# First group of the gated-delta layer: two weight panels and the gate weights read the residual times the norm's weights, and the root is multiplied in behind PSUM

## The reference

```python
x = x + rmsnorm(ff, g_post_mlp)                       # end of the first block (norm "nB")
hn = rmsnorm_2(h, pre_norm[layer])                    # norm "n3": h * rsqrt(mean(h*h) + eps) * pre_norm
proj = hn @ w_in                                      # q, k, v, z (panels) and b, a (gates)
qkv = silu(causal_depthwise_conv(qkv, conv_w))        # four taps per channel
beta = sigmoid(b)
g = -exp(a_log) * softplus(a + dt_bias)               # decays; gc = cumsum(g) within chunks of 64
```

## Time and profile before

| what | value |
|---|---|
| median of 3 runs | 1941.73 us (1940.2 to 1943.67) |
| the profiled execution | 1942.34 us, its span 1939.6 us |
| PE busy | 1833.5 us, 95% of the span |
| DVE, ACT, POOL busy | 994.7, 822.8, 676.4 us |
| the stretch of the change | about 742 to 800 us of the span |

### The profile page before, as it was taken

How to read it: one execution, slowest core, us unless ns; L and a number is a source line. 1 busy time by engine, 2 the same in 40 slices (tenths; PEclk the granted TensorE clock), 3 DMA queues, 4 the chain that set the end, 5 groups by cost and what they waited for, 6 DMA issues and landing times.

```text
span 1939.6 us, 30688 instructions
## 1 busy us (share of the span) xinstructions
PE 1833.5 (95%) x11693; PEld 1538.4 (79%) x11829; DVE 994.7 (51%) x1753; ACT 822.8 (42%) x1503; POOL 676.4 (35%) x429
## 2 busy tenths in 40 slices
PE   6999999999999998998999999999978999999996
PEld 4777788888787876887989998998976667777776
DVE  6522233731111225665765774775766556566666
ACT  4566643352323233633633642562445443333433
POOL 3222244453534342270280263255224212222312
PEclk9999999999999998999999999999999999999998
DMA  5112133232323230420230131122132101221201
GB/s 186 55 55 66 55 98 109 66 98 68 118 80 105 86 99 21 137 79 1 80 89 23 55 91 48 52 80 78 34 111 76 55 33 55 65 55 53 76 32 44
DMA packets 73668, 138.90 MB, mean 72 GB/s; under 512 B 30640, under 2 KB 42416, under 8 KB 73296
## 3 DMA queue, kind: packets, MB, share of 16 engines
q1 hardware_dynamic: 72976, 132.41, 22.7%
q10 hardware_dynamic: 576, 4.87, 0.6%
HBM read 127.62 MB, written 9.63 MB: 71 GB/s over the span
## 4 chain that ended last, share of the span: by engine, by line
PE 44%; DVE 6%; POOL 5%; issue 3%; ACT 3%; DMA 0%; SPq 0%; ACTq 0%; POOLq 0%; DVEq 0%
PE ps L348 9%; PE ps L350 8%; PE ps L349 8%; PE ps L3092 4%; PE ps L3048 2%; POOL wsp L343 2%; PE ps L3055 2%; PE ps L3082 1%; POOL ov L836 1%; PE ps L2770 1%; POOL work L832 1%; PE ps L2874 1%; PE ps L2907 1%; PE ps L2912 1%; DVE aux_f L1789 1%
## 5 line engine op out<-in xcount | busy, mean ns | idle before, releaser
L343 POOL TENSOR_TENSOR wsp<-raw,wsp 128x1024 fp32r<-128x1024 f32 x228 | 549.8, 2418 | 1154.7 <-ACT wsp L338 1154.5
L348 PE MATMUL ps<-h_split,wsp 128*128 128x264 f32 (+2 forms) x1552 | 535.0, 345 | 16.8 <-DVE h_split L497 5.0
L349 PE MATMUL ps<-h_split,wsp 128*128 128x264 f32 (+2 forms) x1552 | 516.0, 332 | 0.0
L350 PE MATMUL ps<-h_split,wsp 128*128 128x264 f32 (+2 forms) x1552 | 515.6, 332 | 0.0
L348 PEld LDWEIGHTS ps<-h_split,wsp 128*128 128x128 f32 x1552 | 294.3, 190 | 58.2 <-issue 17.2
L349 PEld LDWEIGHTS ps<-h_split,wsp 128*128 128x128 f32 x1552 | 295.3, 190 | 28.8 <-issue 0.2
L350 PEld LDWEIGHTS ps<-h_split,wsp 128*128 128x128 f32 x1552 | 294.2, 190 | 29.2
L338 ACT ACTIVATE wsp<-raw 128x1024 fp32r<-128x1024 f32 x228 | 237.6, 1050 | 95.2 <-PE ps L350 94.5
L348 PE MATMUL ps<-y_split,wsp 128*128 128x512 f32 (+2 forms) x512 | 196.4, 384 | 11.5 <-DVE y_split L531 5.3
L349 PE MATMUL ps<-y_split,wsp 128*128 128x512 f32 (+2 forms) x512 | 192.5, 376 | 0.0
L350 PE MATMUL ps<-y_split,wsp 128*128 128x512 f32 (+2 forms) x512 | 192.0, 375 | 0.0
(11 more groups left out here) (391 smaller groups left out, 2929.6 us busy)
## 6 DMA issues: line engine op xcount, KB each, us to landing
raw<-in_w SPq DMA_DIRECT2D x228, 512.0 KB, 3.5
m_home<-ov SPq DMA_DIRECT2D x16, 256.0 KB, 3.5
x_home<-x_res ACTq DMA_DIRECT2D x1, 2112.0 KB, 6.9
x_res<-in_x SPq DMA_DIRECT2D x4, 512.0 KB, 5.3
out<-x_res SPq DMA_DIRECT2D x16, 128.0 KB, 1.7
x_res<-x_home ACTq DMA_DIRECT2D x1, 1584.0 KB, 7.4
mats<-in_mats SPq DMA_DIRECT2D x1, 640.0 KB, 7.4
x_res<-x_home ACTq DMA_DIRECT2D x1, 528.0 KB, 3.9
```

Of the source, the lines that this page charges most:

```text
L343: pool.tensor_tensor(wsp[:, s, 1, :], raw[:, s, :], wsp[:, s, 0, :].bitcast(F32), ALU.subtract).then_inc(lo_ready, 1)
L348: pe.matmul(o, wh, xh, start=start, stop=False)
L349: pe.matmul(o, wh, xl, start=False, stop=False)
L350: return pe.matmul(o, wl, xh, start=False, stop=stop)
```

## The change

The norm "n3" gets two versions. The first is without the root: while `norm_add` still runs, ACT rounds `X` times the norm's weights into `Y` (tile `y_split`; `gained_high`, L526), and DVE makes its correction (`low_plain`, L531) two additions behind. With it PE computes panels 0 and 1 and the gate weights, in between the sums of squares. The root is multiplied in as DVE takes the results from PSUM: `rows_rooted` for the gates, `tile_rooted(0)` and `tile_rooted(1)` for the two tiles, into `QKV` (in tile `work`), from where the taps then read. The second version is with the root, as before, into `HS`, for panel 2 and all behind (`scaled_whole`, `high_whole`, `low_whole`); its small scratch moves from `ov` to `work` (`N3`). The gates' steps stand at other places, ACT's `split_high` of panels 2 and 3 stands between the squares, half of tile 3 stands ahead of the decay rows. Semaphore counts move along.

```diff
--- before.py
+++ after.py
+        N3 = dict(sq=(F[:, 4224:4752], F[:, 4752:5280]), rs=F[:, 6864:7392], tmp=(F[:, 7392:7920], F[:, 7920:8448]))
...
+        ROOTED = (0, 1)
...
-        def norm_add(dve, tag, src, gain, N, c, rs):
+        def norm_add(dve, tag, src, gain, N, c, rs, after=None):
...
+                if after is not None and kt >= 2:
+                    after(kt - 2)
+            if after is not None:
+                after(KT - 2)
+                after(KT - 1)
...
@@ ACT @@
-            norm_squares(act, "n3", lambda k: X[:, k, :], N2, ready=lambda k: added("nB", k))
-            norm_rsqrt(act, "n3", N2, True)
-            norm_high(act, "n3", N2, hs(ALL))
+            for k in range(KT):
+                norm_square(act, "n3", lambda k: X[:, k, :], N3, k, lambda k: added("nB", k))
+                gained_high(act, "n3", k, Y[:, 0, k, :], X[:, k, :], "pre_norm_0")
+                if k in (2, 4):
+                    split_high(act, P_GDN + AHEAD + k // 2 - 1)
+            norm_rsqrt(act, "n3", N3, True)
...
-                split_ahead(0)
                 if first:
-                    gates_front()
-                    split_ahead(1)
-                    gates_middle()
+                    for k in range(KT):
+                        high_whole(k)
+                        if k == 5:
+                            gates_middle()
                     conv_exp(0)
                     decay_high()
...
@@ DVE @@
-            norm_add(dve, "nB", lambda k: acc1[:, k, :], "g_post_mlp", N1, REAL, PS[:, 7, :])
...
-            norm_apply(dve, "n3", lambda k: X[:, k, :], "pre_norm_0", N2, hs(ALL))
+
+            def low_plain(k):
+                gained_low(dve, "n3", k, Y[:, 1, k, :], X[:, k, :], "pre_norm_0", Y[:, 0, k, :])
+            norm_add(dve, "nB", lambda k: acc1[:, k, :], "g_post_mlp", N1, REAL, PS[:, 7, :], low_plain)
...
+            def rows_rooted():
+                dve.wait_ge(sem("ba_pe"), 1)
+                dve.tensor_tensor(two(ba_f[0:32, :]), PS[0:32, 6:8, 0:HALF], two(N3["rs"][0:32, :]), ALU.mult)\
+                   .then_inc(sem("ba_dve"), 1)
+
+            def tile_rooted(t):
+                dve.wait_ge(used, P_GDN + t + 1)
+                dve.tensor_tensor(two(QKV[:, t, :]), acc2(2 * t), two(N3["rs"]), ALU.mult)\
+                   .then_inc(sem("norm_branch"), 1)
...
+                    scaled_whole(0)
+                    scaled_whole(1)
+                    for k in range(2, KT):
+                        low_whole(k - 2)
+                        scaled_whole(k)
+                        if k == 3:
+                            rows_rooted()
+                        if k == 5:
+                            gates_front()
+                            tile_rooted(0)
+                        if k == 6:
+                            gates_end()
+                    low_whole(KT - 2)
+                    low_whole(KT - 1)
                     taps(0)
-                    gates_front()
+                    tile_rooted(1)
                     conv_clamp(0)
                     decay_low()
...
@@ PE @@
-            norm_mean(pe, "n3", N2, True)
...
                     ready(0)
+                    ready(1)
+                    for kt in range(KT):
+                        square_sum(kt)
+                        if kt % 2:
+                            plain(0, kt // 2)
+                            plain(1, kt // 2)
                     for kt in range(KT):
...
-                        last = mm3t(pe, 6, *w, HS, kt, kt == 0, kt == KT - 1)
...
-                        last = mm3t(pe, 0, *part(0, kt), HS, kt, kt == 0, kt == KT - 1)
+                        last = mm3t(pe, 6, *w, Y, kt, kt == 0, kt == KT - 1)
+                    last.then_inc(sem("ba_pe"), 1)
+                    for kt in range(4, KT):
+                        plain(0, kt)
+                    gates_turned()
+                    for kt in range(4, KT):
+                        plain(1, kt)
+                    pe.wait_ge(*rooted(0))
+                    ready(2)
+                    for kt in range(KT):
+                        pe.wait_ge(*whole_ready(kt))
+                        last = mm3t(pe, 0, *part(2, kt), HS, kt, kt == 0, kt == KT - 1)
+                        if kt == 4:
+                            decay_sums()
                     last.then_inc(used, 1)
-                    project(1, 2, 0, 3)
-                    gates_turned()
-                    project(1, 2, 3, 6)
-                    decay_sums()
-                    project(1, 2, 6)
-                    pe.wait_ge(sem("g_conv"), 1)
-                    project(2, 0)
+                    pe.wait_ge(*rooted(1))
+                    project(3, 2, 0, 4)
                     pe.wait_ge(sem("rows_moved"), 16 + 64)
...
                     decay_rows(5, 4).then_inc(sem("g_gr"), 1)
-                    pe.wait_ge(sem("g_conv"), 2)
-                    project(3, 2, 0, 4)
```

95 lines of the change are left out of this document (63 added, 32 removed).

## The result

The changed kernel takes 1953.62 us (median of 9 runs, 1946.81 to 1957.44); the kernel before, on the same chip, 1943.44 (1940.2 to 1947.43). The ratio is 1.0048, with a 95% interval of 1.0037 to 1.0059: slower by 9.3 us, where 4.1 were forecast. All three say slower, each by less than half a per cent; their mean, weighted by their intervals, is 1.0040, 7.8 us. The kernel before itself lies 1.7 to 2.4 us above the 1941.73 from which the forecast counted: that was the median of its first three runs, and samples of 9 to 35 runs give 1943.44 to 1944.12.

A forecast was written before the change was run, and what follows sets the result against it. It took the chain through norm n3 and the decays, not PE, as the bound: root 3.8 us late, collision 4.4, `decay_low` 4.3 late, +4.1 at `l2_scale(1)`, so 1945.8 us. Range 1940.3 to 1949.3.

The forecast's parts named there:

- The corrections and the root: At norm n3: DVE's eight corrections between the additions make POOL's last addition and the root 3.8 us later.
- The collision: First two scalings on DVE wait for POOL's two back-to-back panel splits: 4.4 us, bounds 0 and 4.8.
- above 2 us each: Sign that the forecast is right: each of the first two scalings of `h_split` on DVE takes over 2 us.
- From the second scaling to `decay_low`: DVE's scalings, corrections, gate steps and taps, then conv's exponential on ACT: `decay_low` ends at 785.3, 4.3 us late.
- The decays' way and the first row: The decays' way through DRAM takes 8.56 us as before, so PE's first decay row comes at 793.9.
- PE's clock there: Low clock expected when `l2_sum(0)` starts at 797.3; 5.9 us to `l2_sum(1)`; `l2_scale(1)` ends at 806.4, +4.1.
- Behind it nothing takes the shift back: After `l2_scale(1)`, DVE's queue, M through DRAM and POOL's elimination keep the same steps, so the +4.1 us stays.
- The two waits of PE: Sign that the forecast is right: PE idle 5 us before the decay rows and 2 to 3 behind.
- PE the bound: Rival, chance 0.10: tile 2 ends 4.1 us earlier and the wait for the decays closes; 1937.6, faster.
- No collision: Rival, chance 0.10: scalings run beside the splits, or splits come earlier; all behind 4.4 earlier; 1941.4, no change.
- Slack behind: Rival, chance 0.13: decays are 4 us late, but taps and panels behind have room; 0 to 1.5 us arrive; 1942.5.
- PE slow from the start: Rival, chance 0.07: squares and half tiles leave PE at 1.2 GHz, all is 9 us late; 1950.7.

The follow-up runs named there:

- early splits: Changed kernel with panels 2 and 3 split on ACT and POOL ahead of the norm's additions; median 1943.71 us, ratio interval 0.9994 to 1.0021.
- the delay: Kernel before with seven unused products (4.8 us) more on DVE between the root of n3 and the first scaling; ratio 1.0033.
- decays first: Changed kernel with the decays' small steps ahead of taps and conv's exponential, both groups of Abs ahead of that of tile 1; 1950.28 us.
- matmuls in the wait: Changed kernel with 44 unused matmuls more on PE between the first half of tile 3 and the decay rows; its time is not given in the text.

## Why the prediction was right or wrong

The direction and the mechanism of the stretch were right, the size was not: +4.1 us were forecast, +7.8 measured (+5.6, +7.8 and +9.3 in three measurements). The step that failed is the end of the sum: it takes the +4.1 at `l2_scale(1)`, worked out against one profile, for the whole difference, with the work behind put at +0 ("the same steps"), and adds it to the median of three runs. The runs showed in its place +5.0 at `l2_scale(1)` against that profile, +5.4 against the mean of two, +7.8 in the time, and a start 1.7 to 2.4 above 1941.73.

- *The corrections and the root*: 3.8 late forecast, 3.5 measured. POOL's additions and DVE's corrections held each other up, as foreseen for the last: 1.75 us for POOL's (1.28 in the earlier trace rows), 2.47 for the two corrections beside it (eight took 5.52 where no addition ran). Right in size. But that last addition was one of three, and all took 1.75, not only the last.
- *The collision*: 4.4 forecast; 4.2 by the early splits, which take it away. Here both scalings ended after the second split, as the upper bound said, because the copy of `cwg` took the slot between the splits (2.29 us). The rule of the Trainium skill (SBUF — State Buffer, "SBUF: two separate sides") foretold this order, and the trace agrees with it. The pair ended at (766.9), where the sum had 767.3. Right, and the term that decided; only the sign "above 2 us each" failed, since the copy paid for one of the two waits and the second scaling took 0.76.
- *From the second scaling to `decay_low`*: 785.3 forecast, (785.28) measured. That it is right to 0.1 is in part luck: from the pair's end 18.0 were forecast and 18.3 measured, which made up for the pair's 0.4.
- *The decays' way and the first row*: 793.9 forecast, (794.2). Nearly right: the way through DRAM took 8.8 to 9.0 us in the three profiles instead of 8.56. "This is the step that decides" was only half right: taken forward by 3.6 us, the decays gave back 0.5 to 1.4, because DVE's taps and the ACT work behind them are as late.
- *PE's clock there*: the low level came as forecast, the times with it were a little too small. I had 5.9 us from the start of `l2_sum(0)` to that of `l2_sum(1)`; it was 6.2 (6.4 and 5.7 in the other profiles), and from the first row to `l2_sum(0)` it was 3.78 instead of 3.4 (the prediction's own rows give 3.55). `l2_scale(1)` was forecast at 806.4, and measured (807.3), (807.7) and (806.8).
- *The kernel before as the measure*: I took one profile of it, with the clock lower behind the norm than in its repeat (0.50 against 0.68 from 760 to 764). Against the mean of the two, the stretch is later by 4.9 to 5.8, 5.4 in the mean, instead of 4.1. In the same way its first three runs were a low sample of its time.
- *"Behind it nothing takes the shift back"*: right, shown by the delay. It also doesn't shrink: 4.0 to 4.9 us in the stretch came with a ratio of 1.0033 (+4.1 to +8.7 us).
- *The two waits of PE*, 5 and 2 to 3 us, were 6.36 and 2.98. That nothing lies over the second was right. That this costs was wrong: with the half tile put back there `l2_sum(0)` starts 2.3 later and `l2_sum(1)` at the same time.
- *The rivals.* PE the bound: refuted, PE idled 6.36 ahead of the rows. No collision: refuted by the copy and the pair. Slack behind: refuted by the delay. PE slow from the start: refuted, its clock was 1.00 from 764 to 770, where the kernel before had just come up.

Of +7.8, then, 5.4 are shown in the stretch: 3.0 of them (2.5 to 3.4) are the collision and 1.7 the corrections between the additions, each by the run that takes it away; 0.7 are left with both gone. The other 2.4 are not shown to belong to the change. In the profiles the rest of the run is longer by 1.1 in the mean (1102.2 against 1101.2), with the low clock behind this group as the part that can be pointed at. Two of the three intervals reach below 5.4 (down to 1.0016 and 1.0024, 3.1 and 4.7 us); the first does not (1.0037, 7.2 us), and the three together reach down to some 6.3. The other nine kernels, whose stretch is 0.7 to 6.0 us later than before, have ratios that stand for 0.4 to 6.4 us, in sum 26 us for 28 of shift: about one for one, where the changed kernel has 1.4. Whether a shift of this place brings more low clock behind it on average than by chance stays open; 14 profiles don't settle it. The range I gave, up to 1949.3, holds the last of the three medians and not the other two. It had no room for what the clock adds outside the place of the change: single runs of either kernel spread over 7 to 11 us.

None of the versions was faster than the kernel before; the best, early splits alone or with one of the other edits, are level with it.

## What to carry to other kernels

Before moving a GpSimd operation, look which two-operand SBUF work of VectorE will then stand beside it; here two moved splits cost 4.2 us at the scalings and some 3 at the end of the stretch, and moving them out of the way again cost nothing. A small instruction can take the slot between two long ones and send the large one behind it to the end. When one late step is taken forward, ask for the second that is as late: here 5.6 us at `l2_sum(0)` came out as 0.5 to 1.4 at the end of the stretch. And before a sum of a few us is trusted, take two profiles of the kernel before, and more than three runs: the same code differed by 0.9 us in 96 and by up to 6 in where this stretch began, and the median of three runs lay 1.7 to 2.4 below those of 9 to 35.

## What was not expected of the hardware

- A copy of 128 x 32 elements on DVE took 2.29 us beside a split on POOL, and 0.18 without.
- The first product of `norm_add`, behind identical code, started between 740.94 and 747.01 us in three profiles of the same kernel. The rest of the run behind the stretch took 1099.6 to 1107.0 us.
- POOL's last addition took 1.75 us where DVE's correction had started 0.15 to 0.16 ahead of it (three profiles of the changed kernel), and 1.28 and 1.29 where it had started 0.04 and 0.05 ahead (decays first, matmuls in the wait). A tenth of a microsecond there moved the first scalings by 0.5.
- PE kept busy for 5.51 of the 6.4 us of a wait (clock 1.00) did not keep its clock: it fell to 0.50 in the next wait, of 2.96 us.
